# Neighbourhood attention over 8 x 16 tiles of queries, with a bias table laid out on the host

## The chip, the cores and the metric

The kernel runs on one core of one Trainium2 chip, as one launch. The metric is the device time of that launch in microseconds; lower is better. TensorE multiplies into PSUM (8 banks of 512 fp32 columns for each of 128 partitions), VectorE and ScalarE read PSUM and SBUF, GpSimd works in SBUF, and SyncE issues the weight loads.

## The reference

Two small transformer models of two layers each run one behind the other over 512 latent tokens, seen as a grid of 8 rows by 64 columns, and 256 context tokens. The change touches one operation, the attention of the second layer of the first model. It has 8 heads of 128 features:

```
cols = np.arange(GRID_W)                              # GRID_W = 64
c_start = np.clip(cols - WIN_C // 2, 0, GRID_W - WIN_C)      # WIN_C = 16
col_mask = (cols[None, :] >= c_start[:, None]) & (cols[None, :] < c_start[:, None] + WIN_C)
...
r_start = jnp.clip(r - wr // 2, 0, rows - wr)         # rows = wr = 8, so 0
s_lat = einsum('bhqd,bhrkd->bhqrk', q_r, k_b) * scale + bias
s_lat = where(col_mask[:, None, :], s_lat, -inf)
s_ctx = einsum('bhqd,bhkd->bhqk', q_r, k_ctx) * scale
p = softmax(concatenate([s_lat, s_ctx], -1))
out = p_lat @ v_b + p_ctx @ v_ctx
```

As the grid has 8 rows and the window is 8 rows high, every query sees all 8 rows, in a window of 16 columns that is held inside the grid, and all 256 context tokens. The bias is a table of 15 row distances by 31 column distances for each head. Q and K are normalised over the features before the scores.

## The kernel before

The whole program is written out by hand as one instruction stream for each engine, with semaphores between them. Every product is fp32 in effect: operands are split into a rounded half and a rest (hi and lo), and three matmuls of type fp32r (hi x hi, lo x hi, hi x lo) are added up in PSUM. ScalarE casts each block of weights to its hi half (line 330), GpSimd subtracts to get the lo half (line 390), each into one of two slots. Products of probabilities and V, transposes and sums over partitions are plain fp32, which TensorE does in two passes where it is no transpose.

The stage in question is called near. Its work for one head e is five items and four units.

- An item is a projection: 8 x 3 matmuls into one PSUM bank (`item` and `products`, line 2390). Item 0 is Q over the 512 latent tokens. Items 1 and 2 are K over the 768 tokens in two pieces of 384 columns, items 3 and 4 are V in two pieces of 384. VectorE evicts an item (`evict`, line 2576), ScalarE squares it (2511), TensorE sums the squares over the partitions with a matmul against ones (`post`, 2424), ScalarE takes the root (2520), VectorE takes the reciprocal and scales (`finish`, 2588 and 2589), ScalarE rounds it to hi (2525) and VectorE subtracts to get lo (`low`, 2594). V items are transposed by TensorE instead (2428) and copied (2583).
- A unit u is one tile of 128 queries of a head, two whole rows of the grid, so that u // 4 is the head and u % 4 the tile. TensorE multiplies its scores (2449): 256 context columns into one bank and all 512 latent columns into another. VectorE takes the minimum of the negated scores and adds the bias on the way (`shift`, 2603 and 2604), ScalarE takes the exponential with its sum (2536), VectorE scales by the reciprocal of that sum (`normalise`, 2610 and 2612). TensorE transposes the probabilities, 6 blocks of 128 (`turn`, 2437), ScalarE copies all 768 columns to SBUF (2531), TensorE multiplies the 6 blocks by V (`weigh`, 2460), and VectorE copies the result away (`take`, 2617).

These are interleaved: `step(u)` on TensorE issues the transposes of unit u-1, the scores of unit u and the product with V of unit u-1. The units of head e-1 run between the items of head e: a step follows items 0, 1, 2 and 4. After the last item, steps 28 to 32 run with parts of the output projection between them (line 2371). One bank holds the scores of the context and one those of the latent tokens, for one unit at a time, and the transposes of a unit use two banks.

The bias is made on the chip during head 0. TensorE multiplies a small banded matrix (31 rows) by the transposed table, 128 matmuls in 16 groups (line 2381). VectorE adds the column mask to each group and spreads it in SBUF (line 2568) so that every column of the grid has a row of 120 values, 15 row distances for 8 heads. The table comes by one small DMA (`load_rpb`, on ScalarE's queue).

## Time and profile before

| | us |
|---|---|
| median of 3 runs | 3625.74 |
| lowest and highest of them | 3624.43, 3628.43 |
| span of the profiled execution | 3613.9 |
| TensorE busy in that span | 3486.9 |
| VectorE busy | 1619.4 |
| ScalarE busy | 1223.8 |
| GpSimd busy | 1173.4 |

The span runs from the first to the last instruction of one execution on the chip; the median is over other executions. Busy time of TensorE is that of matmuls, which overlap each other, so a matmul's own duration in a timeline is longer than the distance to the next one; costs are read from the distances of starts. The stage near runs from about 1463 to 1799 us of the span.

### The profile page before, as it was taken

The page shows a single profiled execution, that of the slowest core. Times are in us where ns is not written, and L with a number is a line of the kernel's source. Part 1 is how long each engine was busy: PE and PEld are TensorE (multiplying, and loading weights), DVE is VectorE, ACT ScalarE, POOL GpSimd, SP SyncE. Part 2 cuts the span into 40 slices and gives each one's busy share as a digit, 9 for nine tenths or more (in the row PEclk, how much of TensorE's full clock was granted, in tenths as well). Part 3 has the DMA queues.
Part 4 walks back from the last instruction along what each step waited for, and adds up shares of the span by engine and source line. Part 5 has one row for each costly group of instructions (what it writes and reads, how often), then busy time and mean ns, then how long its engine had stood idle before and what let it go on. Part 6 is the DMA issues. An engine that isn't in the chain of part 4 may idle for free.

```text
span 3613.9 us, 61844 instructions
## 1 busy us (share of the span) xinstructions
PE 3486.9 (96%) x24970; PEld 3053.1 (84%) x24970; DVE 1619.4 (45%) x2762; ACT 1223.8 (34%) x1848; POOL 1173.4 (32%) x812
## 2 busy tenths in 40 slices
PE   8999988889999999999999999999999999999998
PEld 6777878878888888889888888978999999778887
DVE  6966644446220222666662135455512355564121
ACT  4545432233111111455532223255312232542222
POOL 1221122223222233111155454213444432145453
PEclk9999999999999999999999999999999999999999
DMA  5320000001432421111133232112222321123332
GB/s 229 112 70 25 32 2 2 2 25 59 174 110 91 154 86 60 41 42 42 45 96 101 88 104 75 59 48 65 88 93 87 99 70 53 48 76 94 98 93 93
DMA packets 65341, 273.80 MB, mean 76 GB/s; under 512 B 9856, under 2 KB 11008, under 8 KB 62080
## 3 DMA queue, kind: packets, MB, share of 16 engines
q1 hardware_dynamic: 61280, 268.58, 22.4%
q8 instruction: 144, 2.36, 0.3%
q10 hardware_dynamic: 3872, 2.49, 0.2%
q14 instruction: 45, 0.37, 0.0%
HBM read 268.95 MB, written 2.10 MB: 75 GB/s over the span
## 4 chain that ended last, share of the span: by engine, by line
issue 51%; PE 21%; POOL 19%; DVE 6%; ACT 1%; POOLq 0%; PEld 0%; PEldq 0%; DVEq 0%; ACTq 0%
POOL w_lo L390 18%; PE ps L407 10%; PE ps L1488 3%; DVE arena L1776 1%; DVE arena L1762 1%; PE ps L506 1%; PE ps L1998 1%; PE ps L1571 0%; PE ps L2004 0%; DVE arena L1832 0%; PE ps L1549 0%; PE ps L1903 0%; POOLq L385 0%; POOL delta_bufs L2295 0%; DVE arena L1781 0%
## 5 line engine op out<-in xcount | busy, mean ns | idle before, releaser
L390 POOL TENSOR_TENSOR w_lo<-raw,w_hi 128x512 fp32r<-128x512 f32 (+1 forms) x760 | 1101.0, 1469 | 2169.9 <-ACT w_hi L330 2169.9
L330 ACT CAST w_hi<-raw 128x1024 fp32r<-128x1024 f32 (+1 forms) x380 | 419.6, 1104 | 1583.1 <-PE ps L407 1262.7
L407 PE MATMUL ps<-act_hi,w_hi 128*128 128x512 f32 (+2 forms) x2048 | 579.0, 337 | 9.3 <-POOL w_lo L390 3.7
L407 PE MATMUL ps<-act_lo,w_hi 128*128 128x512 f32 (+2 forms) x2048 | 576.8, 336 | 0.0
L407 PE MATMUL ps<-act_hi,w_lo 128*128 128x512 f32 (+2 forms) x2048 | 576.5, 336 | 0.0
L407 PEld LDWEIGHTS ps<-act_hi,w_hi 128*128 128x128 f32 x2048 | 360.1, 188 | 63.3 <-issue 23.5
L407 PEld LDWEIGHTS ps<-act_hi,w_lo 128*128 128x128 f32 x2048 | 362.4, 188 | 41.9
L407 PEld LDWEIGHTS ps<-act_lo,w_hi 128*128 128x128 f32 x2048 | 362.2, 188 | 40.9
L407 PE MATMUL ps<-ff_hi,w_hi 128*128 128x512 f32 (+2 forms) x1056 | 297.1, 336 | 0.0
L407 PE MATMUL ps<-ff_hi,w_lo 128*128 128x512 f32 (+2 forms) x1056 | 297.0, 336 | 0.0
L407 PE MATMUL ps<-ff_lo,w_hi 128*128 128x512 f32 (+2 forms) x1056 | 297.0, 336 | 0.0
L2753 PE MATMUL ps<-act_hi,w_hi 128*128 128x272 f32 (+1 forms) x896 | 265.2, 296 | 0.0
L2753 PE MATMUL ps<-act_lo,w_hi 128*128 128x272 f32 (+1 forms) x896 | 253.8, 283 | 0.0
L2753 PE MATMUL ps<-act_hi,w_lo 128*128 128x272 f32 (+1 forms) x896 | 253.7, 283 | 0.0
L780 DVE TENSOR_TENSOR nscr<-nscr,ps 128x256 f32<-128x256 f32 (+2 forms) x66 | 34.8, 556 | 436.0 <-PE ps L407 436.0
L407 PEld LDWEIGHTS ps<-ff_lo,w_hi 128*128 128x128 f32 x1056 | 186.5, 188 | 21.1
L407 PEld LDWEIGHTS ps<-ff_hi,w_hi 128*128 128x128 f32 x1056 | 186.5, 188 | 20.9
L407 PEld LDWEIGHTS ps<-ff_hi,w_lo 128*128 128x128 f32 x1056 | 186.5, 188 | 20.8
L2753 PEld LDWEIGHTS ps<-act_hi,w_hi 128*128 128x128 f32 x896 | 169.3, 189 | 10.3 <-issue 5.9
L2753 PEld LDWEIGHTS ps<-act_lo,w_hi 128*128 128x128 f32 x896 | 169.4, 189 | 0.9
L2753 PEld LDWEIGHTS ps<-act_hi,w_lo 128*128 128x128 f32 x896 | 169.5, 189 | 0.0
L725 DVE TENSOR_TENSOR nscr<-nscr,ps 128x512 f32<-128x512 f32 (+2 forms) x50 | 26.4, 556 | 315.8 <-PE ps L407 287.5
(495 smaller groups left out, 6249.1 us busy)
## 6 DMA issues: line engine op xcount, KB each, us to landing
raw<-in_gu SPq DMA_DIRECT2D x176, 512.0 KB, 3.5
arena<-in_ada SPq DMA_DIRECT2D x24, 2048.0 KB, 7.8
raw<-in_dn SPq DMA_DIRECT2D x64, 704.0 KB, 4.1
raw<-in_in SPq DMA_DIRECT2D x56, 512.0 KB, 3.5
raw<-in_even_in SPq DMA_DIRECT2D x28, 512.0 KB, 3.5
raw<-in_odd_in SPq DMA_DIRECT2D x24, 512.0 KB, 3.5
raw<-in_out SPq DMA_DIRECT2D x16, 512.0 KB, 3.6
raw<-in_even_out SPq DMA_DIRECT2D x8, 512.0 KB, 3.5
```

What stands on the lines that cost most here:

```text
L330: act.copy(w_hi[:, j, 0:cols], raw[:, j, 0:cols]).then_inc(s["hi_ready"], 1)
L390: ins = pool.tensor_tensor(w_lo[:, j, c], raw[:, j, c], w_hi[:, j, c].bitcast(F32), ALU.subtract)
L407: mm = pe.matmul(ps[:, 2 * j + b, 0:cn], wt[:, j, w], acts[:, k, c0:c0 + cn], start=(k == 0 and wt is w_hi and acts is hi), stop=(k == kt ...
L506: mm = pe.matmul(ps[:, 2 * j + b, 0:cn], wt[:, j, w], acts[:, k, c0:c0 + cn], start=(k == 0 and wt is w_hi and acts is hi), stop=(k == KD ...
L725: ins = dve.tensor_tensor(nscr[:, 1, h0:h0 + hn], nscr[:, 0, h0:h0 + hn], ps[:, 2 + b, 0:hn], ALU.mult)
L780: ins = dve.tensor_tensor(nscr[:, 1, h0:h0 + hn], nscr[:, 0, h0:h0 + hn], ps[:, 2 + b, 0:hn], ALU.mult)
L1488: mm = pe.matmul(ps[:, h, 0:cn], wt[:, b % 2, w], a[:, k, c0:c0 + cn], start=(k == 0 and wt is w_hi and a is act_hi), stop=(k == KD - 1 an ...
L1762: ins = dve.scalar_tensor_tensor(acc, gd[:, m, j:j + GN], v("conv", 5 * m + j), acc, ALU.mult, ALU.add)
L1776: dve_link(dve, n, dve.reciprocal(r, r))
L1998: mm = pe.matmul(pblk(2, d, e, b), blk(DEC_B if l % 2 else LAB_B, d, e, b), blk(X, d, e, b), start=True, stop=True)
L2753: mm = pe.matmul(ps[:, h, 0:cn], wt[:, b % 2, w], a[:, k, TOK2 + c0:TOK2 + c0 + cn], start=(k == 0 and wt is w_hi and a is act_hi), stop=( ...
```

## The change

The tiles of queries, the bias and the items are laid out in another way.

- A unit is now all 8 rows of the grid by 16 columns. Tokens of Q, K and V are reordered on eviction: the 64 columns of the grid are cut into 8 octets, and a head's 512 latent tokens are stored octet by octet, within one octet row by row (`by_octets`, `by_rows`). A tile of 16 columns is then 128 tokens in a row, and the keys that it can see are 4 octets (256 keys) for the two inner tiles and 3 octets (192 keys) for the outer ones.
- The scores of a unit are 256 context and 256 latent columns, both in one bank, with two banks in turn for successive units. The outer tiles multiply 256 latent columns too, of which 192 are read. Exponential and scaling cover 512 or 448 columns.
- The transposes are 4 blocks, in one bank, with two banks in turn. The copy is 512 columns, and the product with V is 4 matmuls. In outer tiles one of these uses 64 rows: half of an octet pair of V (`PIECES`). To make that fit, V's octets are stored rotated by one, so that the eviction of item 4 is two copies.
- K and V are cut at the border of context and latent tokens: items are 512 (Q), 512 (K latent), 256 (K context), 256 (V context), 512 (V latent). A step follows items 0, 1, 3 and 4.
- The bias comes from the host as a table of 128 x 2048 fp32 (1 MB), by one DMA where the small one was. VectorE makes three versions of it in head 0, with the column mask of inner, left and right tiles added: 10 additions of 512 elements. The banded matrix, the 128 matmuls, the 16 additions and their semaphores go. The constants' array is 112 columns narrower.
- VectorE's copy of the result writes it back in the old order of tokens.

```diff
-        THIRD = T // 2
+        NEAR_COLS = (None, (CTX, LAT), (0, CTX), (0, CTX), (CTX, LAT))
+        def by_octets(rows):
+            return rows.rearrange("p (o r j) -> p r o j", o=8, r=8)
+        def by_rows(rows):
+            return rows.rearrange("p (r o j) -> p r o j", o=8, r=8)
+        KEYS = ((0, 192), (64, 256), (192, 256), (320, 192))
+        SCORED = (0, 64, 192, 256)
+        PIECES = (((0, 0, None), (P, 1, None), (CTX - 64, 5, 64), (CTX + 64, 2, None)),
+                  ((0, 0, None), (P, 1, None), (CTX, 2, None), (CTX + P, 3, None)),
...
-            u = 4 * (e - 1) + (i if i < 3 else i - 1)
-            return None if i == 3 or e == 0 else u
+            u = 4 * (e - 1) + (i if i < 2 else i - 1)
+            return None if i == 2 or e == 0 else u
...
-            def bias(g):
...
-                        mm = pe.matmul(ps[64 * h:64 * h + 64, 2 + g % 4, 120 * q:120 * q + 120], band[0:31, 63 - c:127 - c],
-                                       pa[0:31, 1 - h:121 - h], start=True, stop=True)
...
-                for t in range(6):
-                    mm = pe.transpose(ps[:, 4 + t // 4, (t % 4) * P:(t % 4 + 1) * P], near_z[:, u % 2, t * P:(t + 1) * P], ident)
+                for t, (c, _, _) in enumerate(PIECES[u % 4]):
+                    mm = pe.transpose(ps[:, 4 + u % 2, t * P:(t + 1) * P], near_z[:, u % 2, c:c + P], ident)
...
-                for b, (k0, kn) in enumerate(BOTH):
+                for z0, c0, cn in ((0, 0, CTX), (CTX, CTX + SCORED[b], 256)):
                     for q, k in ((q_hi, k_hi), (q_lo, k_hi), (q_hi, k_lo)):
-                        mm = pe.matmul(ps[:, 2 + b, 0:kn], q[:, e % 2, q0:q0 + P], k[:, e % 2, k0:k0 + kn],
+                        mm = pe.matmul(ps[:, 2 + u % 2, z0:z0 + cn], q[:, e % 2, b * P:(b + 1) * P], k[:, e % 2, c0:c0 + cn],
...
-                for t in range(6):
-                    mm = pe.matmul(ps[:, 6, 0:P], near_v[:, e % 2, t, :], near_pt[:, u % 2, t * P:(t + 1) * P],
-                                   start=(t == 0), stop=(t == 5))
+                for t, (_, tile, half) in enumerate(PIECES[u % 4]):
+                    rows = slice(0, P) if half is None else slice(half, half + 64)
+                    mm = pe.matmul(ps[:, 6, 0:P], near_v[rows, e % 2, tile, :], near_pt[rows, u % 2, t * P:(t + 1) * P],
+                                   start=(t == 0), stop=(t == 3))
...
-                act.copy(near_pt[:, u % 2, 0:T], ps[:, 4:6, :].rearrange("p a t -> p (a t)")[:, 0:T]).then_inc(s["near_copied"], 1)
+                act.copy(near_pt[:, u % 2, 0:4 * P], ps[:, 4 + u % 2, :]).then_inc(s["near_copied"], 1)
...
+            def tables(i):
+                whole = near_tables[0][0]
+                if i == 1:
+                    dve.wait_ge(s["rpb_landed"], 16)
+                kind = i % 3
+                table, mask = near_tables[kind]
+                for o in range(table.shape[2]):
+                    cube = lambda a: a.rearrange("p e (r j) -> p e r j", j=8)
+                    ins = dve.tensor_tensor(cube(table[:, :, o]), cube(whole[:, :, o + (1 if kind == 1 else 0)]),
+                                            mask[:, 8 * o:8 * o + 8].unsqueeze(1).unsqueeze(1).to_broadcast([P, 8, 8, 8]), ALU.add)
...
-                dve.tensor_copy(dst, ps[:, item_bank(at), 0:cn]).then_inc(s["item_read"], 1)
+                src = ps[:, item_bank(at), 0:cn]
+                if cn == LAT:
+                    dst, src = by_octets(dst), by_rows(src)
+                if at % ITEMS == 4:
+                    dve.tensor_copy(dst[:, :, 1:8], src[:, :, 0:7])
+                    dst, src = dst[:, :, 0], src[:, :, 7]
+                dve.tensor_copy(dst, src).then_inc(s["item_read"], 1)
...
-                dve.tensor_copy(near_mix[:, e, q0:q0 + P], ps[:, 6, 0:P]).then_inc(s["near_taken"], 1)
+                rows = near_mix[:, e].rearrange("p (r b o j) -> p b r o j", r=8, b=4, o=2)[:, b]
+                dve.tensor_copy(rows, ps[:, 6, 0:P].rearrange("p (o r j) -> p r o j", o=2, r=8)).then_inc(s["near_taken"], 1)
...
-                act.dma_start(pa[0:31, 1:121], dram["rpbT"]).then_inc(s["rpb_landed"], 16)
+                act.dma_start(near_bias, dram["rpb"]).then_inc(s["rpb_landed"], 16)
```

TensorE, the step behind item 1 of head 1, before: the sum of squares of Q, six transposes, the scores, six products with V, and the first matmul of the next item.

```order
L2424 MATMUL ps<-arena,base 128x512
L2437 MATMUL ps<-base,arena 128x128 x6
L2449 MATMUL ps<-near_parts 128x256 x3
L2449 MATMUL ps<-near_parts 128x512 x3
L2460 MATMUL ps<-arena 128x128 x6
L2390 MATMUL ps<-act_hi,w_hi 128x384
```

The same place with the change:

```order
L2418 MATMUL ps<-arena,base 128x512
L2432 MATMUL ps<-base,arena 128x128 x4
L2442 MATMUL ps<-near_parts 128x256 x6
L2454 MATMUL ps<-arena 128x128 x4
L2386 MATMUL ps<-act_hi,w_hi 128x256
```

Two transposes and two products with V are gone, the latent scores are 256 columns, and the item behind the step has 256 columns.

VectorE in head 0, before, from the eviction of item 0 on: evictions (2576), bias additions out of PSUM (2568), reciprocal and scaling of Q, then the same for K's first piece.

```order
L2576 COPY arena<-ps 128x512
L2568 TENSOR_TENSOR arena<-ps,base 128x120x4 x4
L2576 COPY arena<-ps 128x384
L2568 TENSOR_TENSOR arena<-ps,base 128x120x4 x4
L2588 RECIPROCAL arena<-arena 128x512
L2589 SCALAR_TENSOR_TENSOR arena<-arena,vec 128x512
L2576 COPY arena<-ps 128x384
L2568 TENSOR_TENSOR arena<-ps,base 128x120x4 x4
L2588 RECIPROCAL arena<-arena 128x384
L2589 SCALAR_TENSOR_TENSOR arena<-arena,vec 128x384
```

The same stretch with the change, where 2575 is an eviction and 2559 an addition to the bias table:

```order
L2575 COPY arena<-ps 128x8x8x8 x2
L2559 TENSOR_TENSOR arena<-arena,base 128x8x64 x3
L2588 RECIPROCAL arena<-arena 128x512
L2589 SCALAR_TENSOR_TENSOR arena<-arena,vec 128x512
L2575 COPY arena<-ps 128x256
L2559 TENSOR_TENSOR arena<-arena,base 128x8x64 x3
L2588 RECIPROCAL arena<-arena 128x512
L2589 SCALAR_TENSOR_TENSOR arena<-arena,vec 128x512
L2594 TENSOR_TENSOR near_parts<-arena,near_parts 128x512
```

The additions are fewer and read SBUF instead of PSUM, the first three stand behind two evictions, and K's long item comes ahead of the short one.

## Rows read from the trace of the kernel before

**Rows 1.** the page's first line: span and instructions
```profile
span 3613.9 us, 61844 instructions
```

**Rows 2.** busy time by stretch: us, PE PEld DVE ACT POOL, clock, DMA share, GB/s
```profile
1482.00:1506.00 24.00, 23.97 (x262) 21.31 (x257) 17.42 (x21) 4.64 (x8) 3.35 (x3) 0.93 0.16 45
1589.60:1627.40 37.80, 37.80 (x231) 34.14 (x230) 24.54 (x45) 22.41 (x31) 7.67 (x7) 1.00 0.15 42
```

**Rows 3.** timeline of TensorE: start us, us, engine, line, operation
```profile
1632.60 0.82 PE L2437 MATMUL ps<-base,arena 128*128 128x128 f32 x6
1633.17 1.29 PE L2449 MATMUL ps<-near_parts 128*128 128x256 f32 x6
1634.35 1.58 PE L2460 MATMUL ps<-arena 128*128 128x128 f32 x12
1635.68 0.42 PE L2390 MATMUL ps<-act_hi,w_hi 128*128 128x384 f32 x1
```

**Rows 4.** timeline of ScalarE at the same step
```profile
1632.80 0.69 ACT L2520 ACTIVATE arena<-ps,eps_t 128x512 f32<-128x512 f32 x1 [2.92 <-PE ps L2424]
1633.45 0.80 ACT L2531 COPY arena<-ps 128x768 f32<-128x768 f32 x1
```

**Rows 5.** timeline of ScalarE near the program's start
```profile
27.01 0.58 ACT L983 COPY mix<-ps 128x512 f32<-128x512 f32 x1 [2.32 <-PE ps L961]
```

**Rows 6.** timeline of TensorE, two matmuls of 256 columns, later layer
```profile
2202.29 0.28 PE L2753 MATMUL ps<-act_hi,w_hi 128*128 128x256 f32 x1
2202.41 0.28 PE L2753 MATMUL ps<-act_lo,w_hi 128*128 128x256 f32 x1
```

**Rows 7.** timeline of TensorE, heads 0 and 1
```profile
1502.55 3.50 PE L2381 MATMUL ps<-pa,base 31*64 31x120 f32 x64
1505.97 0.50 PE L2390 MATMUL ps<-act_hi,w_hi 128*128 128x512 f32 x1
...
1511.56 0.49 PE L2428 MATMUL ps<-base,arena 128*128 128x128 f32 x3
...
1514.16 0.45 PE L2390 MATMUL ps<-act_hi,w_hi 128*128 128x384 f32 x1 [1.06 <-POOL w_lo L390]
```

**Rows 8.** timeline of VectorE, head 0
```profile
1479.95 0.69 DVE L2576 COPY arena<-ps 128x512 f32<-128x512 f32 x1
...
1487.65 3.34 DVE L2588 RECIPROCAL arena<-arena 128x512 f32<-128x512 f32 x1
1491.03 0.75 DVE L2589 SCALAR_TENSOR_TENSOR arena<-arena,vec 128x512 f32<-128x512 f32 x1
...
1500.80 0.69 DVE L2594 TENSOR_TENSOR near_parts<-arena,near_parts 128x512 fp32r<-128x512 f32 x1
...
1504.45 0.66 DVE L2568 TENSOR_TENSOR arena<-ps,base 128x480 f32<-128x480 f32 x1 [0.16 <-PE ps L2381]
```

**Rows 9.** timelines of GpSimd and VectorE: conversions, and a subtraction under one
```profile
1480.34 2.50 POOL L390 TENSOR_TENSOR w_lo<-raw,w_hi 128x512 fp32r<-128x512 f32 x2 [22.03 <-ACT w_hi L330]
...
1806.35 2.99 POOL L390 TENSOR_TENSOR w_lo<-raw,w_hi 128x512 fp32r<-128x512 f32 x2 [1.71 <-ACT w_hi L330]
...
1808.11 1.77 DVE L560 TENSOR_TENSOR nscr<-nscr 128x512 f32<-128x512 f32 x1
```

**Rows 10.** timelines of TensorE, VectorE and ScalarE, units 29 and 30
```profile
1777.89 0.87 PE L2437 MATMUL ps<-base,arena 128*128 128x128 f32 x6 [0.21 <-DVE arena L2612]
...
1783.15 0.85 PE L2437 MATMUL ps<-base,arena 128*128 128x128 f32 x6 [0.47 <-DVE arena L2612]
...
1780.33 0.75 DVE L2604 CUSTOM_DVE_ANT_0 arena<-ps,arena,small 128x512 f32<-128x512 f32 x1
...
1782.38 0.62 DVE L2612 TENSOR_SCALAR arena<-arena,small 128x768 f32<-128x768 f32 x1
...
1781.12 0.94 ACT L2536 ACTIVATE arena<-arena,small 128x768 f32<-128x768 f32 x1 [1.51 <-DVE small L2604]
```

**Rows 11.** busy time by stretch, behind the bias matmuls
```profile
1488.00:1490.00 2.00, 2.00 (x8) 2.00 (x7) 2.00 (x1) 0.00 (x0) 0.00 (x0) 0.50 0.00 0
```

More of the change, by code:

```diff
@@ L103, in shape_tables @@
     bo64 = (r // 64 == c // 64).astype(np.float64)
-    cmask = np.zeros((P, 64))
-    q = i % 64
-    start = np.clip(q - 8, 0, 48)
-    kk = np.arange(64)[None, :]
-    cmask[:] = np.where((kk >= start[:, None]) & (kk < start[:, None] + 16), 0.0, -BIG)
-    band = np.zeros((P, 128))
-    n = np.arange(127)
-    for j in range(31):
-        band[j, :127] = (78 - n == j)
+    cmask = []
+    for block, first, octets in ((1, -1, 4), (0, 0, 3), (3, -1, 3)):
+        q = 16 * block + 8 * (i // 64) + i % 8
+        start = np.clip(q - 8, 0, 48)[:, None]
+        kk = 16 * block + 8 * first + np.arange(8 * octets)[None, :]
+        cmask.append(np.where((kk >= start) & (kk < start + 16), 0.0, -BIG))
     dmask = np.where(c <= r, 0.0, -BIG)
-    base = np.concatenate([ident, np.ones((P, P)), bo64, cmask, band, dmask], 1)
+    base = np.concatenate([ident, np.ones((P, P)), bo64] + cmask + [dmask], 1)
     inv = 10000.0 ** (-np.arange(16, dtype=np.float32) / np.float32(16))
@@ L2489, in pe_near @@
                         post(3)
-                        for g in range(12, 16):
-                            bias(g)
                     if e and near_order(e, i) is not None:
@@ L2597, in shift @@
             def shift(u):
[L2598 removed]
+                _, b, k0, kn, table = near_unit(u)
                 dve.wait_ge(s["near_scores"], u + 1)
@@ L2623, in dve_near @@
                     evict(at)
-                    if e == 0:
-                        for g in range(4 * i, min(4 * i + 4, 16)):
-                            bias(g)
+                    if e == 0 and 1 <= i <= 3:
+                        tables(i)
                     if u is not None:
@@ L3488, in kp, with near_table @@
         return z.reshape(-1, P, z.shape[-1]).transpose(1, 0, 2)
+    def near_table(z):
+        wide = np.zeros((8, 15, 47), np.float32)
+        wide[:, :, 8:39] = z
+        rows = [wide[:, 7 - r:15 - r, 15 - 8 * o - j:47 - 8 * o - j] for o in range(2) for r in range(8) for j in range(8)]
+        return np.stack(rows).reshape(P, 8, 8, 4, 8).transpose(0, 1, 3, 2, 4).reshape(P, 2048)
     ew, ow = a["even_w_in"][0], a["odd_w_in"][0]
```

103 lines of the change are left out of this document (42 added, 61 removed).

## The prediction

> **What bounds the kernel now.** I read the page first: one profiled execution spans 3613.9 us [rows 1], and the median of the timed runs is 3625.74 us, so 11.8 us lie around the span; I take them as unchanged, and a microsecond off the span is one off the median. Only the neighbourhood attention is touched, some 345 us of the span. The table of stretches comes next: one head costs 37.8 us, in which TensorE is busy for all 37.80 and the clock is full, while VectorE works 24.54, ScalarE 22.41 and GpSimd 7.67 [rows 2]. TensorE therefore sets the pace of seven of the eight heads, and what is taken from it there is won, until something else is late. In the stretch of head 0 TensorE is busy too (23.97 of 24.00), but with the 128 bias matmuls, and its clock is 0.93 [rows 2]. Last comes the timeline of a step, which says what a step waits for, and the timeline of the end, where no projection is left as cover.
>
> **A step of attention (32 of them).** Between two projections TensorE transposes the probabilities of the last tile (6), multiplies scores (6) and multiplies by V (6, two passes each). The rows read 1632.60, 1633.17, 1634.35 and 1635.68 [rows 3]: 0.57 us, 1.18 us and 1.33 us. By part:
> - Transposes, 6 to 4: 0.57 x 2/6 = 0.19 us less.
> - Products with V, 6 to 4: 1.33 x 2/6 = 0.44 us less. In the edge tiles one of the four has 64 rows; I give that nothing, since its 128 columns stream as before.
> - Scores, 3x256 and 3x512 to 6x256. A 256-column matmul starts every 0.12 us [rows 6], so the six are issued in 0.72 us. But the product with V does not start when the scores are out: it waits for ScalarE's copy of the transposes. The copy runs from 1633.45 for 0.80 us, to 1634.25, and the product starts at 1634.35 [rows 3, 4]. The copy shrinks from 768 to 512 columns, and a copy of 512 from PSUM takes 0.58 us [rows 5]. So from the start of the scores to the product it is now 0.28 + 0.59 + 0.10 = 0.97 us, not 0.72: the gain is 0.21 us and not 0.46.
>
> Sum: 0.19 + 0.21 + 0.44 = 0.84 us a step. In one step of four it is less. Behind the query item ScalarE first takes the root over 512 columns, 1632.80 to 1633.49 [rows 4], and the transposes will now be done at about 1633.26. The copy can't start before the root ends, so the 0.19 of the transposes is lost again behind it: the product starts some 0.2 us earlier than today in all, and with its own 0.44 this step saves about 0.65 us. Steps 1 to 27 run under projections, 7 of them of this kind: 7 x 0.65 + 20 x 0.84 = 21.4 us. Bounds: nothing of the scores gained, 27 x 0.63 = 17 us; all of it as the columns say, 27 x 1.09 = 29 us. I take the chain of the copy, because its end and the product's start stand 0.10 us apart.
>
> **The items.** Q, K and V of a head were 512 and 4 x 384 columns, and are 512, 512, 256, 256, 512: 2048 both times and as many matmuls, so nothing. But the step after K's first third moves behind a projection of 512 columns, and no step follows the short K item. The steps are then at least 5.5 us apart, which gives VectorE more time between scores and the next transposes. A 512-column item takes 5.59 us, from 1505.97 to 1511.56 [rows 7], a 256-column one 24 x 0.12 = 2.9 us [rows 6]. Where it is tight: the sum of squares of the short K item waits for a root, a rounding, a weight cast and a square, one after the other on ScalarE. I put these at 3.6 us from the sum of squares before it (an estimate from the durations of the same operations at 512 columns), while TensorE arrives after 3.7. I allow 0.3 us in all for misses.
>
> **VectorE in a head.** Shift and reduction over 512 local keys take 0.75 us [rows 10] and now cover 256 or 192; the scaling over 768 takes 0.62 [rows 10] and now covers 512 or 448. Four steps save about 4 x 0.45 = 1.8 us; the second copy of the last V eviction adds 0.15. That is 23 us of a head of 34.5: covered. The evictions and the take are now permuted in chunks of 8. The bias addition of today reads PSUM in an even more broken order, 480 elements in 0.66 us [rows 8], and a plain eviction of 512 takes 0.69 [rows 8], so a permuted order costs nothing by these rows. The Trainium skill, SBUF - State Buffer (the remark on cachelines under "Door 1: The DMA port swizzle"), says instead that accesses which leave their 16-byte line of SBUF pay, and that PSUM's lines hold 8 bytes. By that the bias addition should have been slow, and the trace does not agree. Chunks of 8 elements would pay less than it; what a penalty would do here is worked out below as the slower rival.
>
> **Head 0.** Away go 128 matmuls on TensorE, which is 3.50 us for each run of 32 (64 passes) [rows 7] and 14 us in all, and 16 additions of 0.66 us on VectorE [rows 8]. In come 10 additions of 512 elements, both operands in SBUF, on VectorE alone. An addition or subtraction of that kind takes 0.69 us [rows 8], 0.60 to the next one, and 1.77 us while GpSimd converts weights [rows 9]. The table of 1 MB is sent off where the small one is now, 27 us before it is needed; to be late it would have to move at under 39 GB/s, less than the mean over a stretch with long pauses (45 GB/s, the last column of [rows 2]). Head 0 is then no longer bound by TensorE but by VectorE, and I follow it:
> - 1479.95, where the norm ends as before [rows 8]; two evictions to 1481.2; three additions, the first under GpSimd's conversion of 1480.34 to 1482.84 [rows 9], to 1484.1.
> - Reciprocal 3.34 and scaling 0.75 for Q [rows 8], 4.0 us with their overlap, to 1488.1; eviction 0.35; three additions, of which I let one fall under the next conversion, to 1491.3.
> - The same 4.0 us for K's long item, to 1495.3; subtraction and eviction 0.95, four additions 2.4, to 1498.7; the short K item 2.2, to 1500.9.
> - ScalarE rounds it (0.4) and casts the weights of the next K item (1.0); GpSimd converts them (2.5 [rows 9]): 1504.8.
>
> TensorE needs those weights for the second item of head 1. It started that item at 1514.16, after 1.06 us of waiting for just this conversion [rows 7]; now at about 1504.9. Its own work (two K/V items, three sums, the next Q item) ends at 1501.7 by the same rates and is not the last. Gain 9.3 us. If an addition of this shape costs 1.1 us to the next one instead of 0.6, 10 x 0.5 = 5 us are lost, and the gain is 4.5; if GpSimd disturbs none, it is 11.
> The Trainium skill, VectorE: DVE Perf Modes ("Two Vector instructions with no wait between them"), says that the second tensor of an operation with two SBUF inputs is read through an interface shared with GpSimd. The 1.77 us row agrees. Were all ten under a conversion, they would cost 10 us more than in my sum; GpSimd converts here for only 2.5 us in each eight or so.
>
> **The end.** From step 28 on the steps form one chain: scores, shift, exponential, scaling, transposes. Two turns stand 5.26 us apart: 1777.89 to 1783.15 [rows 10]. Off it come: transposes 0.19; scores 0.32, since nothing but their end counts here; shift 0.27 to 0.33 (0.75 for 512 columns [rows 10], now 256 or 192); exponential 0.22, as for the copy (0.94 at 768 columns [rows 10]); scaling 0.15 to 0.2. Together 1.2 us, four times: 4.8 us. TensorE's own work in such a turn (0.4 + 0.97 + 0.9 + two parts of the output projection, 1.4) is 3.7 us, inside the 4.06 that are left. The last step has no scores and saves 0.8 us.
>
> **Sum.** 21.4 - 0.3 + 9.3 + 4.8 + 0.8 = 36 us. The span goes to 3578 us and the median to 3625.7 - 36 = 3589.7, say **3590 us**.
>
> **Rivals.**
> - VectorE or ScalarE becomes late inside the heads. For it: the slack of 0.1 us in the short K item, and the reciprocals of 3.3 us in front of each scaling. Against it: 23 us of work in 34.5. If each of seven heads waits 1 us and the additions of head 0 cost 1.1 us: 36 - 7 - 5 = 24 us, 3602 us.
> - TensorE's clock. After the bias matmuls, small and narrow, it stood at 0.50 of full speed, which is 1.2 GHz, around 1488 to 1490 [rows 11]. Those matmuls go, but TensorE now idles in gaps between 1474 and 1503, for up to 3 us at a time. Should the clock stay low for all of it, three items (3 + 5.5 + 5.5 us) take twice as long and TensorE is the bound of head 0 again: item 2 of head 1 at about 1516, the 9.3 us gone and 1.5 lost, 3601 us. A drop of 3 us costs below 1 us, as VectorE is later than TensorE there.
> - The scores' whole 0.46 us is gained, since the copy isn't what is waited for: 27 x 0.25 = 7 us more, 3583 us.
> - Slower: permuted access costs several times as much. Evictions (0.69 + 4 x 0.55) and takes (4 x 0.28) are 4.0 us a head. VectorE becomes the bound of a head and undoes the gain once 23 + 4.0 x (s - 1) passes 37.8, so from a factor s of 4.7 on; at a factor of 7 a head takes 47 us and the kernel about 3625 - 9 + 7 x 9 = 3680 us. The bias addition in [rows 8] speaks against any factor.
> - That no time is saved at all, because TensorE is not the bound: its row of 37.80 in 37.80 excludes it nearly.
>
> **How the numbers follow.** Forecast (27 to 43 us gained) 0.80; late VectorE or ScalarE 0.09; clock 0.05; the full gain of the scores 0.03, inside the range at its low end; slower by permuted access 0.02; nothing 0.01. The range: high end 3601, to the two rivals above; low end 3582, the scores' full gain and an undisturbed VectorE in head 0. 0.2% of this kernel is 7.3 us, about what a measurement tells from no change; all cases but the last two lie beyond it: faster 0.96, same 0.02, slower 0.02.
>
> **What would show it.** In a step under projections: transposes 0.38 us to the scores, the product with V 0.97 us after the scores' start, with TensorE idle for 0.2 us before it, and 0.89 us to the next item. A head of 34.5 us. In head 0: additions of 0.69 us, more under GpSimd; the second item of head 1 starting near 1505. At the end turns 4.1 us apart. Wrong would be: additions or evictions above 0.9 us outside GpSimd's work, waits of TensorE for the sum of squares of the short K item or for the probabilities, or a granted clock of 0.5 over more than one item.

## The result

The changed kernel takes 3589.3 us (median of 4 runs, 3586.3 to 3590.1), the kernel before 3625.1 us (4 runs, 3621.6 to 3628.4): a ratio of 0.9904, 95% interval 0.989 to 0.992. It is 35.8 us faster. The forecast was 3590.0 us, in a range of 3582 to 3601.

The spans of the two profiled executions differ by less: 3613.9 us [rows 1] against this first line of the page of the changed kernel.

```profile
span 3587.6 us, 60934 instructions
```

That is 26.3 us, and the reason is not what lies around the span. In each timed run with its span, of either kernel, 2 us lie around it. The eleven runs of the kernel before that were timed beside the experiments go from 3614.4 us, at a mean granted clock of 0.996, to 3632.5 us at 0.990, and its profiled execution (clock 0.995) lay near the lower end. Single executions of one kernel differ by up to 18 us, then. In the traces of the experiments below, the stage without its first part repeats within 0.2 us where nothing in it was edited, and the first part within about 1 us, so most of the spread arises in code that the change doesn't touch. So what follows is read within the stage, from anchor to anchor; for the kernel before there is one trace, so its first part too is known only to about 1 us. The anchors are, in TensorE's timeline, the first product of the stage, the second item of head 1, the last product of head 7 and the first one of the output projection, first before and then after (columns: start us, us, engine, line, operation).

```profile
1462.98 0.48 PE L2390 MATMUL ps<-act_hi,w_hi 128*128 128x512 f32 x1
...
1765.97 0.34 PE L2390 MATMUL ps<-act_hi,w_lo 128*128 128x384 f32 x1
...
1798.81 0.47 PE L425 MATMUL ps<-act_hi,w_hi 128*128 128x512 f32 x1 [0.26 <-DVE act_lo L916]
```

```profile
1466.75 0.48 PE L2386 MATMUL ps<-act_hi,w_hi 128*128 128x512 f32 x1
...
1508.76 0.40 PE L2386 MATMUL ps<-act_hi,w_hi 128*128 128x512 f32 x1
...
1742.88 0.40 PE L2386 MATMUL ps<-act_hi,w_lo 128*128 128x512 f32 x1
...
1769.06 0.47 PE L421 MATMUL ps<-act_hi,w_hi 128*128 128x512 f32 x1
```

With the item at 1514.16 of [rows 7] they give three parts:

| part of the stage | before | after | gain | forecast |
|---|---|---|---|---|
| stage's start to the second item of head 1 (head 0) | 51.18 | 42.01 | 9.2 | 9.3 |
| from there to the last product of head 7 (26 steps) | 251.81 | 234.12 | 17.7 | 20.2 |
| from there to the output projection (step 27, the end) | 32.84 | 26.18 | 6.7 | 6.4 |
| stage | 335.83 | 302.31 | 33.5 | 36 |

The forecast's column splits its sum of 36: 26 of the 27 steps lie in the second part (7 x 0.65 + 19 x 0.84 - 0.3), the last one in the third. Of the experiments, those that leave the heads and the end alone repeat the second part within 0.2 us (234.1 to 234.3) and the last within 0.1 (26.2), but the first varies from 40.9 to 42.1 us in kernels that have the same code there.

The medians fell by 35.8 us and the stage by 33.5. That the median came so close to the forecast is in part luck: the stage gained 2.5 us less than the sum of 36, and the other 2.3 us are within the spread of single runs. The load of the 1 MB table, which was not tried by itself, costs nothing that the traces show: it lands 4.8 us after its issue, and the stretch from the same VectorE instruction to the stage's start is 90.23 us before and 90.21 after, with the load inside it.

**A head**, in the table of stretches of the changed kernel (us, PE PEld DVE ACT POOL, clock, DMA share, GB/s), against the 37.80 us of [rows 2]:

```profile
1611.63:1646.70 35.07, 34.88 (x208) 29.58 (x206) 24.95 (x46) 17.76 (x28) 7.72 (x6) 1.00 0.15 46
```

It takes 35.07 us, where 34.5 were expected. TensorE is still busy for all but 0.2 us of it, and VectorE has 10 us to spare. In TensorE's timeline, first the step behind Q's sum of squares (edge tile 0), then the one behind the short K item's sum of squares (inner tile 1), each up to the next item:

```profile
1620.64 0.95 PE L2442 MATMUL ps<-near_parts 128*128 128x256 f32 x6
1621.75 1.52 PE L2454 MATMUL ps<-arena 128*128 128x128 f32 x8 [0.16 <-issue]
1623.02 0.36 PE L2386 MATMUL ps<-act_hi,w_hi 128*128 128x256 f32 x1
...
1630.15 0.60 PE L2432 MATMUL ps<-base,arena 128*128 128x128 f32 x4
1630.50 0.96 PE L2442 MATMUL ps<-near_parts 128*128 128x256 f32 x6
1631.47 1.13 PE L2454 MATMUL ps<-arena 128*128 128x128 f32 x8
1632.36 0.48 PE L2386 MATMUL ps<-act_hi,w_hi 128*128 128x512 f32 x1
```

Starts alone matter here, since ends are modelled. From the transposes (L2432) to the scores (L2442) it is 0.35 us, from the scores to the product with V (L2454) 0.97 us, behind Q's sum of squares 1.11, and from the product with V to the next item 0.89 us (1631.47 to 1632.36) or 1.27 us (1621.75 to 1623.02). That last difference, between 0.89 and 1.27 us, was not in the forecast. It goes by tiles: inner tiles (four pieces of 128 rows) take 0.89 us, edge tiles (one piece of 64 rows) 1.25 to 1.27 us.

**ScalarE** at the second of these steps. The copy starts at 1630.79 and lasts 0.59 us; the product with V starts 0.09 us behind its end:

```profile
1630.79 0.59 ACT L2517 COPY arena<-ps 128x512 f32<-128x512 f32 x1
```

**Head 0**: TensorE's three waits, then VectorE's three groups of additions, with Q's reciprocal behind the first, and GpSimd's first conversion.

```profile
1485.15 1.12 PE L2418 MATMUL ps<-arena,base 128*128 128x512 f32 x2 [0.77 <-ACT arena L2497]
1487.13 0.39 PE L2386 MATMUL ps<-act_hi,w_hi 128*128 128x256 f32 x1 [0.85 <-POOL w_lo L386]
...
1494.34 0.71 PE L2418 MATMUL ps<-arena,base 128*128 128x256 f32 x2 [3.21 <-ACT arena L2497]
...
1484.95 3.27 DVE L2559 TENSOR_TENSOR arena<-arena,base 128x512 f32<-128x512 f32 x3
1488.15 3.34 DVE L2588 RECIPROCAL arena<-arena 128x512 f32<-128x512 f32 x1
...
1492.53 1.89 DVE L2559 TENSOR_TENSOR arena<-arena,base 128x512 f32<-128x512 f32 x3
...
1499.31 2.48 DVE L2559 TENSOR_TENSOR arena<-arena,base 128x512 f32<-128x512 f32 x4
...
1484.14 2.94 POOL L386 TENSOR_TENSOR w_lo<-raw,w_hi 128x512 fp32r<-128x512 f32 x2 [22.03 <-ACT w_hi L326]
```

Three additions take 3.27 us under GpSimd's conversion, three take 1.89 us and four 2.48 us without it: 0.63 us each where nothing disturbs. TensorE waits 0.77, 0.85 and 3.21 us in this head. The normalisation that feeds the head's first products sets the first 17 us in both kernels: VectorE's first eviction starts 16.97 us behind the stage's start before, and 16.99 us after the change (1483.74). The whole gain lies behind that point.

**The end**: turns start at 1747.59, 1752.54, 1756.61, 1760.63 and 1764.53. The first and two of the others, with the wait that made the first one long:

```profile
1747.59 0.60 PE L2432 MATMUL ps<-base,arena 128*128 128x128 f32 x4
1748.88 0.98 PE L2442 MATMUL ps<-near_parts 128*128 128x256 f32 x6 [0.69 <-DVE near_parts L2594]
...
1756.61 0.60 PE L2432 MATMUL ps<-base,arena 128*128 128x128 f32 x4
...
1760.63 0.63 PE L2432 MATMUL ps<-base,arena 128*128 128x128 f32 x4 [0.20 <-DVE arena L2613]
```

These last two are 4.02 us apart, for 5.26 of [rows 10] and 4.06 expected. The first is 4.95 long: the scores of tile 28 wait 0.69 us for the rounding rest of the last K item, which VectorE computes under a conversion of GpSimd in 1.49 us.

### The profile page after: what moved, and what is told of

Its sections match the earlier page's. It is cut to its first block, busy times and chain, and to the rows that moved or that the text cites. A ratio compares the mean times of both kernels' runs of the same rounds, so it can differ in the third digit from the quotient of the medians.

```text
span 3587.6 us, 60934 instructions
## 1 busy us (share of the span) xinstructions
PE 3456.5 (96%) x24522; PEld 3010.5 (84%) x24522; DVE 1619.0 (45%) x2764; ACT 1190.0 (33%) x1834; POOL 1174.4 (33%) x812
## 4 chain that ended last, share of the span: by engine, by line
issue 51%; PE 22%; POOL 19%; DVE 6%; ACT 1%; POOLq 0%; PEld 0%; PEldq 0%; DVEq 0%; ACTq 0%
POOL w_lo L386 18%; PE ps L403 10%; PE ps L1484 3%; DVE arena L1772 1%; DVE arena L1758 1%; PE ps L502 1%; PE ps L1994 1%; PE ps L1567 1%; PE ps L2000 0%; DVE arena L1828 0%; PE ps L1545 0%; POOLq L381 0%; POOL delta_bufs L2291 0%; DVE arena L1777 0%; PE ps L1555 0%
## 5 line engine op out<-in xcount | busy, mean ns | idle before, releaser
L721 DVE TENSOR_TENSOR nscr<-nscr,ps 128x512 f32<-128x512 f32 (+2 forms) x50 | 26.3, 555 | 315.8 <-PE ps L403 287.5
```

Source lines behind the costliest of these rows:

```text
L721: ins = dve.tensor_tensor(nscr[:, 1, h0:h0 + hn], nscr[:, 0, h0:h0 + hn], ps[:, 2 + b, 0:hn], ALU.mult)
```

## The experiments

Each is an edit of the changed kernel. Where a whole time is given, it is the median of 4 or 6 runs, but single runs of one kernel spread over up to 12 us, so what is concluded rests on the traces.

### The row range of V's products

```diff
-                    rows = slice(0, P) if half is None else slice(half, half + 64)
+                    rows = slice(0, P)
```

> Against the changed kernel, whose two timelines show: a product with V of an inner tile (four pieces of 128 rows) is followed by the next item after 0.89 us, one of an edge tile (three of 128 rows, one of 64) after 1.25 to 1.27 us. Here the piece of 64 rows is multiplied with all 128; the output is then wrong in the edge tiles, since 64 probabilities of the context meet 64 rows of V that are not theirs. Theory: the narrower row range itself costs 0.36 us, so all products take 0.89 us, a head falls from 35.07 to 34.35 us, and with 13 edge tiles under projections and one on the last chain 14 x 0.36 = 5 us go: 3584.3. Rival: the 0.36 us belong to the position (the step behind a Q or a V item, its DMA or its ScalarE work) and stay: 3589.3.

Measured: 3584.1 us, ratio to before 0.989 (0.987 to 0.991). The product with V in the step behind Q's sum of squares (edge tile 0), and the next item:

```profile
1621.11 1.13 PE L2454 MATMUL ps<-arena 128*128 128x128 f32 x8 [0.16 <-issue]
1622.00 0.36 PE L2386 MATMUL ps<-act_hi,w_hi 128*128 128x256 f32 x1
```

The product with V of an edge tile takes 0.89 us as all others do. The second part of the stage is 228.88 us, for 234.12: 5.2 us less, the whole stage 5.6 us less. The theory holds: it is the row range that costs, and not the position in the head.

What in the 64 rows costs the time was read from a second kernel, in which tile 1 has four pieces of 64 rows and tile 2 two:

```diff
+                    if u % 4 == 1 or (u % 4 == 2 and t >= 2):
+                        half = 0
                     rows = slice(0, P) if half is None else slice(half, half + 64)
```

> The changed kernel with three arrangements of row ranges in the product with V, to be read in one trace (the output is wrong, since these pieces leave out 64 rows). Tiles 0 and 3 as they are: one piece of 64 rows, third (rows 64 to 127) or fourth (rows 0 to 63) of four, 1.25 us to the next item. Tile 1: all four pieces of rows 0 to 63. Tile 2: the last two of rows 0 to 63. All-128 takes 0.89 us. If a piece of 64 rows costs 0.36 us more each, tile 1 takes 0.89 + 4 x 0.36 = 2.3 us and tile 2 1.6 us. If it is the change from one row range to the other that costs, 0.18 us for each (the weight load of the next piece can't run ahead of it), tile 1 and tile 2 both take about 1.25 us, since each has one change in and one out. The first makes the kernel some 16 us slower, the second some 5 us.

The products with V of tile 1 and tile 2 in its timeline, each with the next item's or the next product's start:

```profile
1629.46 1.13 PE L2456 MATMUL ps<-arena 64*128 64x128 f32 x8
1630.52 0.50 PE L2386 MATMUL ps<-act_hi,w_hi 128*128 128x512 f32 x1
...
1637.64 1.32 PE L2456 MATMUL ps<-arena 128*128 128x128 f32 x8
1638.89 0.50 PE L2386 MATMUL ps<-act_hi,w_hi 128*128 128x512 f32 x1
```

Two pieces of 64 rows cost as much as one (1.25 us), and four cost less (1.06 us, 0.17 above four of 128). The second part of the stage grows by 3.7 us, not by 16. So the piece itself costs nothing; the change of the row range costs, about 0.18 us in each direction if both cost the same. Why four pieces pay only half is not settled; the likely reason is that the change into them falls into the time in which the product waits for the copy anyway, 0.25 us in this step: the product starts 0.96 us behind the scores, as with 128 rows. That wasn't tried by itself, and what in TensorE makes the change cost time no run here shows.

### The copy in front of V's products

```diff
-                    for q, k in ((q_hi, k_hi), (q_lo, k_hi), (q_hi, k_lo)):
-                        mm = pe.matmul(ps[:, 2 + u % 2, z0:z0 + cn], q[...], k[...], start=..., stop=...)
+                    mm = pe.matmul(ps[:, 2 + u % 2, z0:z0 + cn], q_hi[...], k_hi[...], start=True, stop=True)
```

> The changed kernel with two of a step's six score matmuls; the four with a low part are left out, so the scores are coarser. Theory: the product with V waits for ScalarE's copy, 0.97 us behind the start of the scores (1.11 behind Q's root), so leaving out 4 x 0.12 = 0.48 us of scores gains nothing under the projections, and TensorE's waiting before the product grows to 0.7 us; on the chain of the end, where the scores are waited for, 4 x 0.48 = 1.9 us go: 3587.4. Rival: TensorE's own work is the limit, and all 31 steps with scores give 0.48 us: 15 us, 3574.5.

Measured: 3589.5 us, 0.990 (0.989 to 0.992). TensorE behind the short K item's sum of squares:

```profile
1630.97 0.48 PE L2441 MATMUL ps<-near_parts 128*128 128x256 f32 x2
1631.94 1.13 PE L2453 MATMUL ps<-arena 128*128 128x128 f32 x8 [0.49 <-issue]
1632.83 0.48 PE L2386 MATMUL ps<-act_hi,w_hi 128*128 128x512 f32 x1
```

With a third of the score matmuls the product with V still starts 0.97 us behind them, now with 0.49 us of waiting (0.7 expected). The second part of the stage is 234.24 us, as before (234.12), and 1.05 us go at the end (1.9 expected). What comes last in a step is the copy, and the rival by which the scores would give their full 0.46 us is out.

The other side of this: if the product is moved out of the copy's way, the wait should be won.

```diff
                     for k in range(KD):
                         products(e, i, k)
+                        if k == 0 and held:
+                            weigh(held.pop())
...
-                if u:
+                if u and later:
+                    held.append(u - 1)
+                elif u:
                     weigh(u - 1)
```

> The changed kernel with the product with V moved behind the first three matmuls of the next item, in the 26 steps under projections that have one behind them. Theory: TensorE waits before the product for the copy, 0.97 - 0.72 = 0.25 us in an ordinary step and 1.11 - 0.72 = 0.39 us behind Q's root; behind the item's first matmuls (0.69 us at 512 columns, 0.36 at 256) the copy is done, and the wait goes: 20 x 0.25 + 6 x 0.39 = 7.3 us, 3582. Rival: the 0.97 us are the scores' own time (fill and drain), the copy only ends then by chance: nothing, 3589.3. Third: breaking up an item costs TensorE as much as it gains, 0.1 to 0.3 us a step: 3584 to 3590.

Measured: 3583.8 us, 0.988 (0.987 to 0.990). The same step:

```profile
1629.24 0.96 PE L2444 MATMUL ps<-near_parts 128*128 128x256 f32 x6
1630.04 0.40 PE L2386 MATMUL ps<-act_hi,w_hi 128*128 128x512 f32 x1
...
1630.73 1.05 PE L2456 MATMUL ps<-arena 128*128 128x128 f32 x8
1631.54 0.47 PE L2386 MATMUL ps<-act_hi,w_hi 128*128 128x512 f32 x1
```

Scores take 0.80 us, three products of the item 0.69, the product with V 0.81. Against 0.97 and 0.89 that is 0.25 us in all. The second part of the stage is 227.12 us, 7.0 less, where 7.3 were expected. So breaking up the item costs nothing that these distances show.

### Edge tiles with full pieces, same output

```diff
+        PAD = {0: (CTX, CTX + 64), 3: (CTX + 192, CTX + 256)}
-        PIECES = (((0, 0, None), (P, 1, None), (CTX - 64, 5, 64), (CTX + 64, 2, None)),
+        PIECES = (((0, 0, None), (P, 1, None), (CTX, 5, None), (CTX + P, 2, None)),
...
+                if b in PAD:
+                    dve.memset(z[:, PAD[b][0]:PAD[b][1]], BIG)
...
-                z = near_z[:, u % 2, 0:CTX + KEYS[u % 4][1]]
+                z = near_z[:, u % 2, 0:2 * CTX]
```

> The changed kernel, and the same output: the edge tiles get 64 more columns of probabilities, set by VectorE before the scores come to a value whose exponential is zero, so that each of their four pieces has 128 rows. Theory of the first run: the 0.36 us of the row range go as there, 5 us; VectorE's write (about 0.1 us) lies before its wait for the scores and costs nothing under the projections; at the end exponential and scaling of two edge tiles are 64 columns longer, 0.1 us each: 3584.5. Rival: it is the position, then nothing is won and 0.3 us lost: 3589.6.

Measured: 3584.8 us, 0.990 (0.988 to 0.991). VectorE at an edge tile: the write lies in front of a wait for the scores.

```profile
1611.40 0.11 DVE L2604 MEMSET arena<- 128x64 f32 x1
1612.34 0.42 DVE L2608 TENSOR_SCALAR_CACHE_REDUCE arena<-ps 128x256 f32<-128x256 f32 x1 [0.82 <-PE ps L2443]
```

The second part of the stage is 229.09 us, 5.0 less; the last three turns of the end are 0.1 us longer (4.18, 4.15 and 3.98 for 4.07, 4.02 and 3.90), where 0.1 us in each of two edge tiles was expected, but the last part of the stage stays as it was (26.19 us). The stage takes 296.19 us.

### Head 0

```diff
-            table = near_tables[{0: 1, 3: 2}.get(b, 0)][0]
+            table = near_tables[0][0][:, :, 0:kn // 64]
...
-                    if e == 0 and 1 <= i <= 3:
-                        tables(i)
```

> The changed kernel without the ten table additions of head 0; the tiles read the unmasked table, so the output is wrong. The prediction had VectorE's chain set the pace of head 0, with TensorE's own work ending 3.2 us earlier: by that, 3.2 us go (second item of head 1, measured from the stage's start, at 38.7 instead of 41.9 us). Rival, from the timeline of the changed kernel: the sum of squares of the short K item is waited for (3.21 us), that item is evicted behind the reciprocal and scaling of Q, and the reciprocal waits for ScalarE's root until 1487.01, 1.14 us before it now starts; so the additions cost TensorE only 1.1 us and the rest of its wait stays: 40.8 us, and 3588.

Measured: 3589.7 us, 0.990 (0.988 to 0.992). TensorE's long wait, without any addition:

```profile
1497.01 0.67 PE L2418 MATMUL ps<-arena,base 128*128 128x256 f32 x2 [2.64 <-ACT arena L2497]
```

Head 0 takes 41.51 us for 42.01. The repeats of this part differ by about 1 us, so this alone doesn't tell 0 from 1.1, but it is not the 3.2 us of the forecast's chain. That chain ends with GpSimd's conversion: here it ends 38.78 us behind the stage's start, for 41.55 with the additions, so 2.8 us went from it, and the item behind it came only 0.5 us earlier. VectorE's chain was not the last one. The wait of 2.64 us for the short K item's square is there without the additions.

What the first three additions cost TensorE stays open between 0 and 1.1 us, since the clock moved as well. In this kernel it is at 0.50 from 1485.9 to 1492.6; Q's sum of squares takes 1.53 us to the next item for 1.13, ScalarE's root ends 21.35 us behind the stage's start for 20.26, and so the reciprocal starts at 21.4 us in both. In return the last item of the head, which the changed kernel ran at a low clock in 7.26 us, takes 5.68 us.

The reverse, matmuls put back and additions left as they are:

```diff
                     elif i == 2:
+                        filler(2)
                         post(0)
+                        filler(4)
                     elif i == 3:
                         post(1)
+                        filler(4)
                         post(2)
                     elif i == 4:
                         post(3)
+                        filler(4)
```

> The changed kernel with 112 idle matmuls (31 rows, 64 by 120 columns, as the removed bias ones, of which there were 128) put back in head 0 where those stood: 16 ahead of Q's sum of squares, 32 behind it, 32 behind the next, 32 behind the first half of V. Nothing else changes, no additions come with them. Theory: they take 0.109 us each, 12.2 us, of which 4.8 us fall into waits that TensorE has there (0.77, 0.85 and 3.21 us): the second item of head 1 is 7.4 us later, at 49.3 us from the stage's start, and the kernel at 3596.7. Rival: the gain of head 0 came from VectorE's 16 additions, and the matmuls hide in TensorE's waits: 3589 to 3591.

Measured: 3602.4 us, 0.993 (0.992 to 0.995). The second and third of the four groups, and the stretch from 1494 to 1498:

```profile
1491.25 6.66 PE L2470 MATMUL ps<-base 31*64 31x120 f32 x64
...
1503.35 3.50 PE L2470 MATMUL ps<-base 31*64 31x120 f32 x64
...
1494.00:1498.00 4.00, 4.00 (x41) 3.70 (x37) 3.96 (x6) 0.00 (x0) 0.00 (x0) 0.50 0.00 0
```

Head 0 is 53.68 us long, 11.7 more than after the change, and 2.5 more than before it. The direction is the theory's, its 7.4 is too small. The missing 4.3 us are the clock: from 1487.8 to 1501.4 it stands at 0.50, the lower of its two levels, and the 64 passes that take 3.42 us in full (1503.35 to 1506.77) take 6.60 us (1491.25 to 1497.85). The first two groups, Q's sum of squares and the item behind them take 6.4 us more than at the full clock. The changed kernel loses 1.7 us in the same way (below), so the clock took more from this kernel than from either of the others, and its 11.7 us are no clean price of the matmuls.

Then another order in head 0:

```diff
...
-                        post(2)
                     elif i == 4:
+                        post(2)
                         post(3)
...
-                    if e == 0 and 1 <= i <= 3:
-                        tables(i)
+                    if e == 0 and i == 3:
+                        tables(1)
...
+                    if u == 0:
+                        tables(2)
+                        tables(3)
```

> The changed kernel, same output, with head 0 in another order: TensorE takes the last item of head 0 ahead of the sum of squares of the short K item instead of behind it; of the additions, the three of tile 0 come after the last eviction but one, the other seven in head 1 behind the first scaling. Theory: the wait of 3.21 us goes, and so does the low clock of the item behind it (7.26 us instead of 5.56); then VectorE's chain (two reciprocals of 3.34 us, one of 1.75) is last, with the second item of head 1 some 3.5 us earlier, at 38.4 us from the stage's start: 3585.8. Rival: TensorE's clock sinks elsewhere in the head and takes it back: 3589.

Measured: 3590.4 us, 0.991 (0.989 to 0.992), where 3585.8 was expected: the whole time is no shorter than the changed kernel's 3589.3. The clock in the six runs was 0.990 to 0.993, and their spread of 8 us is wider than the gain that the trace shows. Head 0:

```profile
1488.53 0.79 PE L2386 MATMUL ps<-act_hi,w_hi 128*128 128x512 f32 x1
...
1494.42 0.60 PE L2418 MATMUL ps<-arena,base 128*128 128x256 f32 x2
...
1502.65 0.97 PE L2442 MATMUL ps<-near_parts 128*128 128x256 f32 x6 [0.74 <-DVE near_parts L2594]
1503.80 0.50 PE L2386 MATMUL ps<-act_hi,w_hi 128*128 128x512 f32 x1 [0.17 <-POOL w_lo L386]
```

The wait of 3.21 us is gone, and the last item of head 0 runs in 5.89 us (1488.53 to 1494.42) instead of 7.26. The low clock is not gone, it came earlier: 0.50 from 1482.5 to 1485.8, where Q's sum of squares and the short V item, waits left out, take some 1.2 us more than in the changed kernel. The rival had that much right. Head 0 takes 39.29 us, 2.7 less; now TensorE waits 0.74 us for VectorE's subtraction and 0.17 us for GpSimd's conversion, the chain that the forecast had put last.

### The permuted copies

```diff
-                if cn == LAT:
-                    dst, src = by_octets(dst), by_rows(src)
...
-                dve.tensor_copy(rows, ps[:, 6, 0:P].rearrange("p (o r j) -> p r o j", o=2, r=8)).then_inc(s["near_taken"], 1)
+                dve.tensor_copy(near_mix[:, e, b * P:(b + 1) * P], ps[:, 6, 0:P]).then_inc(s["near_taken"], 1)
```

> The changed kernel with plain evictions of the 512-column items and a plain take, in place of those that permute in chunks of 8 (so the output is wrong: the tiles are then 2 rows by 64 columns of keys and queries with the new mask). Theory: a permuted copy costs nothing on VectorE; evictions of 512 columns take 0.69 us and takes 0.28 us in both, the last V item's one copy of 0.69 us replaces 0.62 + 0.21 us, a head stays at 35.07 us, the stage at 302.3 us. Rival: the chunks cost VectorE something, and plain copies are shorter than 0.65 and 0.25 us; under the projections that is hidden all the same, and at the end 0.03 us a step would show.

VectorE's groups by shape (line, engine, operation, tiles, shapes, count | busy us, mean ns | idle time), from 1540 to 1740 us, changed kernel first:

```profile
L2575 DVE COPY arena<-ps 128x512 f32<-128x512 f32 x12 | 8.3, 691 | 32.3 <-PE ps L2386 32.3
...
L2619 DVE COPY arena<-ps 128x128 f32<-128x128 f32 x22 | 6.2, 280 | 0.0
```

```profile
L2570 DVE COPY arena<-ps 128x512 f32<-128x512 f32 x17 | 11.8, 692 | 34.0 <-PE ps L2386 34.0
...
L2613 DVE COPY arena<-ps 128x128 f32<-128x128 f32 x23 | 6.5, 281 | 0.0
```

Permuted or plain, 0.69 and 0.28 us. The stage is 302.13 us for 302.31.

### Together

The three edits (late product with V, full pieces, order of head 0) in one kernel.

> The changed kernel with the late product with V, the padded edge tiles and the new order of head 0 together, same output. If the three act in different places they add up: 5.8 us (difference of the two traces from 1600 us to 1650 us, taken to the stage), 4.9 us and 3.5 us, 14 us in all: 3575. If a step that is 0.6 us shorter makes VectorE or ScalarE late inside a head (TensorE then waits for probabilities or for the short K item's square), it is less, 3578 to 3582.

Measured: 3578.7 us (3576.2 to 3584.9), ratio to before 0.987 (0.985 to 0.989). Its stage takes 287.64 us, 14.7 less than the changed kernel's: 2.8 in head 0 (39.22 us), 11.9 in the heads (222.20 us), nothing at the end (26.22 us). The parts add up, VectorE and ScalarE are not late at a head of 33.2 us (from the scores at 1593.72 to those at 1626.93):

```profile
1600.00:1640.00 40.00, 40.00 (x245) 35.04 (x244) 30.05 (x62) 20.46 (x33) 10.51 (x8) 1.00 0.13 41
```

This kernel is faster than both, the one before and the changed one.

## The forecast, step by step

- **The span and the median.** The 11.8 us that it took for work around the span are a spread of the runs; 2 us lie around it. The forecast subtracted from the median, so nothing came of it.
- **Transposes and scores of a step.** Right: 0.35 us (0.38 expected) and 0.97 us, with the copy as what comes last. Behind Q's sum of squares 1.11, where the root's end holds the copy, as described (1.16 expected). The experiment with two score matmuls shows it.
- **Products with V.** 0.44 us was right for inner tiles (1.33 to 0.89). The sentence "In the edge tiles one of the four has 64 rows; I give that nothing, since its 128 columns stream as before" is the step that failed. What the runs show in its place: in edge tiles the gain is 0.07 us, since 0.36 us are lost to the change of row range, in 13 of the 26 steps of the second part, 4.7 us. Small terms in the other direction (0.23 us a step for the transposes instead of 0.19, 1.11 us instead of 1.16 behind Q's sum, nothing of the allowed 0.3 used, 0.04 us a head in the items) return some 2 us. The full-row kernel gives 5.2 us back.
- **The items.** Right. All items and sums of squares or transposes of V of a head are 25.34 us in all, 25.38 before, and no sum of squares of a short K item was waited for inside heads 1 to 7.
- **VectorE in a head, permuted copies.** Covered, as said, though at 24.95 us busy and not 23: scaling takes 1.44 us in place of 0.45 where GpSimd converts beside it. The forecast read the Trainium skill, SBUF - State Buffer (the remark on cachelines under "Door 1: The DMA port swizzle"), as a price for chunks of 8 as well. But by that remark two accesses to a line of 16 bytes are enough for the full bandwidth, and a chunk of 8 fp32 elements is two whole lines, so it needn't cost anything in SBUF. The trace agrees with that, 0.69 us in either order.
- **Head 0.** The gain of 9.3 us came out (9.2), its chain did not. The forecast had VectorE last and TensorE done 3.2 us earlier. In fact TensorE was in the chain: it waits 3.21 us for the square of the short K item, and then runs the next item at a low clock, 7.26 us for 5.56. The eviction of the short K item stands behind Q's reciprocal on VectorE (to 1492.61), and the square behind the rounding of Q and a weight cast of 1.04 us on ScalarE (to 1493.87). GpSimd's conversion ended in time for the same point by accident (1508.30 for an item that starts at 1508.76). The account that fits, an estimate from the distances of starts: 14.0 us of matmuls and 0.5 us of scores gone, 3.8 us of new waits in the three places and at the last weights (4.83 for 1.06), and 1.4 us of waits for VectorE's norm between the first products, where bias matmuls stood (TensorE busy for 16.34 of 18 us from 1466 on, for 17.76 of 18 in the same stretch before): 9.3 us, for 9.2 measured. The clock took about as much before (at 0.50 from 1487.7 to 1491.1) as after, where it took 1.7 us. That additions slow down under GpSimd was right in kind (three in 3.27 us instead of 1.89). This fits the interface shared with GpSimd through which, by the Trainium skill, VectorE: DVE Perf Modes ("Two Vector instructions with no wait between them"), the second of two SBUF inputs is read; the page has no price. The three slow additions hold Q's reciprocal back by 1.14 us behind the end of the root, but they did not make VectorE's chain the last one.
- **TensorE's clock.** The rival's drop was there, from 1494.9 to 1498.2:

```profile
1494.00:1498.00 4.00, 3.67 (x10) 2.96 (x11) 3.96 (x3) 0.66 (x2) 2.77 (x2) 0.60 0.01 5
```

It cost 1.7 us, more than the "below 1 us" of the forecast, since VectorE was not later than TensorE there. The rival's case, low over three items, did not come.
- **The end.** Turns of 4.07, 4.02 and 3.90 us, as forecast (4.06). The one of 4.95 us was missed, and so was the gain of the first (6.26 to 4.25). Together with step 27 the part gives 6.7 us for 6.4.

So in the heads and at the end the mechanism was right, and the sum 2.5 us too large, by the edge tiles' 4.7 us less some 2 us of small terms. In head 0 the size came out by luck: its chain was wrong.

## What to carry to other kernels

When work between two long matmul groups shrinks, find the other engine's operation that ends last there before you count columns: here a copy of 0.59 us set 0.97 us, and moving the consumer behind three matmuls of the next group won more than cutting four matmuls. Give the pieces of an accumulated product one row range, and fill the rest with zeros, when another engine has room for it (5.0 us in the heads here). And a total that agrees doesn't prove its chain: take the presumed bottleneck out once and see whether the time follows.

## What was not expected of the hardware

- A change of row range between matmuls (128 to 64 rows and back) costs TensorE some 0.36 us, even if only one piece of 128 columns lies between; two neighbouring pieces of 64 rows cost no more, four cost 0.17. The Trainium skill, TensorE: Matmul & The Clock Gate ("Why this matters for your kernels"), says that a single matmul over few rows takes the time of one over 128. For the matmul alone the runs agree, since a second piece of 64 rows beside the first costs nothing more; the price of the change is not in that sentence.
- Scaling 448 columns in SBUF by a value of each row (one tensor input) takes VectorE 0.45 us, and 1.44 us while GpSimd converts. It isn't only operations with two SBUF tensors that suffer:

```profile
1751.82 0.45 DVE L2613 TENSOR_SCALAR arena<-arena,small 128x448 f32<-128x448 f32 x1
...
1614.85 1.44 DVE L2613 TENSOR_SCALAR arena<-arena,small 128x448 f32<-128x448 f32 x1
```

- In head 0 the granted clock fell to 0.50, the lower of its two levels, once in each kernel, at a different place each time. In the kernel before it was low from 1487.7 to 1491.1, with TensorE busy throughout; in the changed kernel from 1494.9 to 1498.2, falling half a us behind the end of a wait of 3.21 us; in the kernel without additions from 1485.9 to 1492.6, falling behind gaps of 0.29 us between products and ahead of the wait of 0.62 us; and from 1487.8 to 1501.4 in the one with 112 narrow matmuls, where TensorE was busy throughout. It cost TensorE between some 1.2 us (new order of head 0) and 6.4 us (narrow matmuls). Where it falls is probably what keeps head 0 from repeating to better than 1 us: of the kernels with the same code there, the one with full pieces, in which it was low from 1484.6 to 1491.4 and full again behind the long wait, has the shortest head 0 (40.91 us).
